# Operands ordered by first use, a residual load moved in the queue, and a ring of four weight slots, in a two-layer decoder trunk

## The chip, the cores and the metric

The kernel runs on one core of a Trainium2 chip. The metric is the device time of one execution in microseconds (us). The core has five engines that run their own instruction streams and wait for each other by semaphores: TensorE (PE, matmuls and transposes, into PSUM), VectorE (DVE), ScalarE (ACT), GpSimd (POOL), and SyncE (SP), which here only issues DMAs, in the order of its program.

## What is computed

Two layers, on 1024 prompt positions and 8 x 8 sample positions (1088 rows of 1024 features), all in fp32:

```python
for l in range(2):
    h = x @ w_in                                   # 1024 -> 1792
    A = gelu(h_u) * (tril(W_s) @ LN(gelu(h_v)) + b)  # gMLP gating in chunks of 128, 8 heads
    B = sliding-window attention, 8 query heads / 2 kv heads, rotary, sinks
    x = LayerNorm(alpha * x + concat(A, B) @ w_out)
    up = x @ w_up                                  # 1024 -> 2 * 2816
    g, u = causal depthwise conv, width 3 (up)
    x = LayerNorm(alpha * x + (gelu(g) * u) @ w_down)   # 2816 -> 1024
```

Outputs are x and the updated key, value, conv and gMLP rows.

## The kernel before

fp32 products are made of three passes with rounded operands: each operand is split into a high half (ACT copies it to fp32r) and a low half (DVE or POOL subtracts the high half from the original), and PE does high x high, high x low and low x high. So each weight tile passes through DMA, ACT, DVE or POOL, and PE. The order of every engine is written out by hand; an instruction behind a wait waits too.

A layer has these stages.

- Input projection, w_in. SP loads pairs of weight tiles (`pair_in`, 1 MB), ACT makes the high half (`hi_in`, L770), POOL the low one (`lo_in`, L682). The first two tiles are multiplied in `two_chunks` (L1702) for each third of the columns. The columns come from row tiles that PE turns (`turn_x`, L1660) into the banks that `x_bank` names (L336), and ACT and DVE evict from there as high and low half (`x_hi` L794, `x_lo` L1153). In layer 0 the odd tiles have banks of their own; in layer 1 all use banks 6 and 7, so each waits for the eviction of the one before. `hi_in` of layer 1 stands at the end of ACT's loop over the down-projection (L1143), behind the square roots of the last norms (`deviation`).
- Gating and attention, which the change doesn't touch.
- Output projection, w_out. Row tiles in three groups, `C3 = [(0,1,2), (3,4,8), (5,6,7)]`. For each of 8 weight rows kk, PE multiplies the three tiles of the group with the high half (two passes) and then the low half. The last two weight rows of a group (kk = 6, 7) are handled tile by tile, so that the three tiles are done one after the other (L1942 to L1953); before the first of them PE waits for both high and both low halves, and in group 0 does the sample values (`samp_values`). DVE adds the residual (`summed`, L1165), which SP brings with `x_rows` (L456); the one of the third tile is issued between weight rows (L626). Then the norm: `deviation` (ACT), `scaled` (DVE), `normal` (ACT), PE turns the tile (`turn_z`), ACT and DVE evict it with gain and bias (`turned`).
- Up-projection, w_up, in 22 slices. Each is seven products of 4 k-tiles by 544 columns (a Strassen-like scheme: 7 products for 8), in the order B_11, B_12, B_S2, B_S1, B_S3, B_22, B_S4. Their right operands are `ba` and `bt`: the x tiles and four sums t1 to t4 of tile halves, each as high and low. For a tile of 4 to 7 they are made in three parts: part 0 is t1 and t2 (used by S2 and S1), part 1 is t3 and t4 (S3 and 22), part 2 the tile itself (S4). ACT's `operand_hi` (L836) does the three parts of a tile together, DVE's `operands` (L1255) turns a tile, makes its sums and its three low parts, and goes to the next tile. The weight blocks go through `block_hi` (ACT), `lo_up` and `sum_up` (POOL; from slice 1 on some through `block_lo`, DVE). After B_11, ACT copies the product out of PSUM (`snap`, L882); for slice 0 this waits for the last low part, because the place it is written to still holds the x tiles. DVE joins the products (`joined`, L1274).
- Down-projection, w_down: three groups of three row tiles in order, each of 22 units (k-tiles), so 66 units d. `down_hi`/`down_lo` split the weight row into slot `dn_slot(d)` (L141), `act_hi`/`act_lo` split the activations, which come back from HBM (`araw<-a_scr`). The last two units of a group are handled tile by tile. Slots 0 and 1 are also the places of the w_in tiles of the next layer and, like slot 3, of blocks of the up-projection. ACT's `down_hi` waits for the unit that used the slot before:

```python
def dn_slot(d):
    return d % 4 if d < DNU - 2 else d - (DNU - 4)      # DNU = 66: units 64, 65 in slots 2, 3
...
name, count = used_d(l, d - (4 if d < DNU - 2 else 2))
```

SP's queue begins with the four constants, x tiles 0 to 2, the first w_in pair and the other x tiles (L393, L516 to L522).

Of the kernel before, what the change touches and what calls it, by code (L numbers as in the profile page):

```python
# [10 lines left out]
ALU = mybir.AluOpType  # L11
# [113 lines left out]
def xo_n(l, t, part):  # L125

    n = sum(parts(u) for u in CORD[:CORD.index(t)])
    return l * sum(parts(u) for u in CORD) + n + part + 1


def ts_n(l, t, i):

    n = sum(0 if u < HK else 4 if u < NB else 8 for u in CORD[:CORD.index(t)])
    return l * 4 * (HK + 2) + n + i + 1
# [6 lines left out]
def dn_slot(d):  # L141

    return d % 4 if d < DNU - 2 else d - (DNU - 4)
# [10 lines left out]
def trunk(nc, x_prompt, x_sample, cache_k, cache_v, cache_conv, w_in, gmlp_g, gmlp_b, w_spatial,  # L154
# [4 lines left out]
    with ctx:  # L159
# [53 lines left out]
        bh_off = [hi_off[i // 2] + 2048 * (i % 2) for i in range(4)] + [e_off + 2048 * i for i in range(3)]  # L213
        bl_off = [lo_off[i // 2] + 2048 * (i % 2) for i in range(4)] + [e_off + 6144 + 2048 * i for i in range(3)]
# [60 lines left out]
        gu = [at(f"gu{i}", [P, 2, UWX], u_off + 9152 * i) for i in range(2)]  # L275
        hg = [at(f"hg{i}", [P, CV], u_off + 18304 + 4416 * i) for i in range(2)]
# [18 lines left out]
        for n in ("const_landed x_landed0 x_landed1 x_landed2 x_landed3 x_tr x_hi x_lo par_landed cs_landed bd_landed bd_zero par_tr "  # L295
# [63 lines left out]
        def half(f, which, h):  # L359

            return gu[f % 2][:, which, HW_ * h:HW_ * h + HW_].rearrange("p (b n) -> p b n", b=2)

# [29 lines left out]
        def _(sp):  # L392
            for dst, src in ((ident[:], c_ident), (mask[:], c_mask), (smask[:], c_smask), (selS[0:HEADS, :], c_sel)):  # L393
                sp.dma_start(dst, src).then_inc(S["const_landed"], 16)
# [121 lines left out]
            for b in range(NB + 1):  # L516
# [3 lines left out]
                if b == 3:  # L520
                    pair_in(0, 0)
                sp.dma_start(xin[b % XS][0:tokens(b), :], src).then_inc(S[f"x_landed{b % XS}"], 16)  # L522

            def body(l):
# [3 lines left out]
                else:  # L528
                    sp.wait_ge(S["z_tr"], l * NTOK)
                    sp.wait_ge(S["z_out2"], 48 * l)  # L530
                    for dst, src in ((mask[:], c_mask), (smask[:], c_smask), (selS[0:HEADS, :], c_sel)):
                        sp.dma_start(dst, src).then_inc(S["const_landed"], 16)
# [82 lines left out]
                for cache, o in ((cache_k, o_ks), (cache_v, o_vs)):  # L615
                    sp.dma_start(o[l, :, 0:WINDOW - DS].rearrange("b s k d -> b s (k d)"),
                                 cache[l, :, DS:WINDOW].rearrange("b s k d -> b s (k d)")).then_inc(S["c_out"], 16)
                for g in range(3):
                    for kk in range(KD):
# [6 lines left out]
                        if g == 0 and kk == 5:  # L626
# [1477 lines left out]
```

## Time and profile before

| | |
|---|---|
| median of 3 runs | 2487.73 us (2486.95 to 2490.62) |
| profiled execution | 2495.53 us, span 2493.8 us |
| PE busy | 2291.3 us, 92% |
| DVE / ACT / POOL busy | 68% / 39% / 29% |
| mean granted PE clock | 0.964 |

The busy share of PE in 40 equal slices, with its granted clock (tenths of full speed; slices of 62 us) and the DMA engines' share:

```profile
PE   6999888699999999999979998886999999999997
...
PEclk9999989799999999999989999898999999999998
DMA  5311135122222225665442212451222222255762
```

Busy counts a matmul that runs at half clock as fully busy. The slices in which PE is below 9 are the start, the attention and output projection of each layer, the turn between the layers (slice 21) and the end. The up-projection of a layer takes about 450 us, its down-projection about 290.

### The profile page before, as it was taken

The numbers are of one execution on the slowest core, as the hardware profiler recorded it, in microseconds if no ns is written. First come the engines' busy times: TensorE is split into PE (matmuls) and PEld (weight loads), VectorE is DVE, ScalarE is ACT, GpSimd is POOL, SyncE is SP. The second block draws the span as 40 slices with busy tenths as digits, with TensorE's granted clock in tenths as the row PEclk, the third lists the DMA queues.
The fourth block names the chain that finished last, engine by engine and source line by source line (L and its number), as shares of the span: only waits on it lengthen the run. The fifth ranks groups of instructions, "written<-read, shape, count | busy, mean of one in ns | idle before, by whom it ended". The sixth has DMA issues, their size and how long they took to land.

```text
span 2493.8 us, 36152 instructions
## 1 busy us (share of the span) xinstructions
PE 2291.3 (92%) x14396; PEld 2038.8 (82%) x14396; DVE 1683.4 (68%) x2092; ACT 983.0 (39%) x1773; POOL 716.6 (29%) x396
## 2 busy tenths in 40 slices
PE   6999888699999999999979998886999999999997
PEld 6997566699999998787779976666999999977875
DVE  1469736677777776776535797376777777757665
ACT  2226625434343344333222266344433444433331
POOL 1110134344444440220211112344444444302211
PEclk9999989799999999999989999898999999999998
DMA  5311135122222225665442212451222222255762
GB/s 143 88 53 38 60 118 170 59 68 65 80 79 80 79 63 179 233 213 194 131 108 62 49 39 85 123 152 43 80 80 79 63 71 79 96 204 197 238 201 80
DMA packets 207975, 269.52 MB, mean 108 GB/s; under 512 B 31952, under 2 KB 166584, under 8 KB 207736
## 3 DMA queue, kind: packets, MB, share of 16 engines
q1 hardware_dynamic: 207808, 267.21, 35.0%
q8 instruction: 115, 1.88, 0.3%
q14 instruction: 52, 0.43, 0.1%
HBM read 217.39 MB, written 46.13 MB: 106 GB/s over the span
## 4 chain that ended last, share of the span: by engine, by line
PE 57%; DVE 19%; ACT 6%; issue 5%; DMA 5%; POOL 5%; SPq 2%; DVEq 0%; ACTq 0%; POOLq 0%
PE ps L1970 21%; PE ps L1690 15%; PE ps L1656 8%; PE ps L1912 6%; DMA wblk<-in_w_up 3%; DVE rl L1340 2%; POOL bl L697 2%; SPq L510 2%; PE ps L1715 1%; DMA wrow<-in_w_down 1%; POOL wblk L705 1%; DVE bl L1272 1%; ACT bh L880 1%; DVE al L1347 1%; DVE Sb L1486 1%
## 5 line engine op out<-in xcount | busy, mean ns | idle before, releaser
L1970 PE MATMUL ps<-bt,bh 128*128 128x272 f32 x3520 | 595.1, 291 | 32.0 <-issue 23.8
L1970 PEld LDWEIGHTS ps<-bt,bh 128*128 128x128 f32 x3520 | 500.4, 190 | 39.6 <-issue 25.4
L880 ACT ACTIVATE bh<-wblk 128x512 fp32r<-128x512 f32 x308 | 183.5, 624 | 547.2 <-POOL wblk L709 234.0
L1970 PE MATMUL ps<-bt,bl 128*128 128x272 f32 x1760 | 365.6, 289 | 0.0
L1272 DVE TENSOR_TENSOR bl<-wblk,bh 128x512 fp32r<-128x512 f32 x210 | 165.4, 804 | 192.2 <-ACT bh L880 192.2
L1970 PEld LDWEIGHTS ps<-bt,bl 128*128 128x128 f32 x1760 | 276.9, 190 | 0.0
L1690 PE MATMUL ps<-rh,ah 128*128 128x512 f32 (+1 forms) x792 | 249.5, 396 | 22.1 <-DVE rzd L1175 6.8
L697 POOL TENSOR_TENSOR bl<-wblk,bh 128x512 fp32r<-128x512 f32 x98 | 166.8, 1707 | 321.4 <-ACT bh L880 321.4
L1690 PE MATMUL ps<-rh,al 128*128 128x512 f32 (+1 forms) x792 | 246.6, 393 | 0.0
L1690 PE MATMUL ps<-rl,ah 128*128 128x512 f32 (+1 forms) x792 | 246.0, 392 | 0.0
L1970 PE MATMUL ps<-ba,bh 128*128 128x272 f32 x1408 | 237.5, 291 | 6.7 <-POOL bl L697 1.7
L1340 DVE TENSOR_TENSOR rl<-wrow,rh 128x1024 fp32r<-128x1024 f32 x132 | 189.4, 1435 | 68.8 <-ACT rh L938 68.8
L1970 PEld LDWEIGHTS ps<-ba,bh 128*128 128x128 f32 x1408 | 198.4, 188 | 15.5 <-DVE gu L1295 13.0
L693 POOL TENSOR_TENSOR rl<-wrow,rh 128x1024 fp32r<-128x1024 f32 x48 | 116.9, 2438 | 307.6 <-ACT rh L792 191.5
L1690 PEld LDWEIGHTS ps<-rh,ah 128*128 128x128 f32 (+1 forms) x792 | 143.1, 184 | 64.6 <-issue 12.5
L1656 PE MATMUL ps<-xh,wh 128*128 128x384 f32 (+1 forms) x576 | 193.9, 337 | 0.9 <-POOL wl L685 0.9
L1656 PE MATMUL ps<-xh,wl 128*128 128x384 f32 (+1 forms) x576 | 190.0, 330 | 0.0
L1656 PE MATMUL ps<-xl,wh 128*128 128x384 f32 (+1 forms) x576 | 189.8, 330 | 0.0
L1912 PE MATMUL ps<-rh,mrow 128*128 128x512 f32 (+1 forms) x576 | 155.7, 413 | 34.2 <-DVE rzc L1175 22.5
L722 POOL TENSOR_TENSOR rzd<-rzd,gain 128x1024 f32<-128x1024 f32 (+1 forms) x18 | 50.6, 2809 | 438.3 <-DMA rzd<-z_scr 438.3
L1690 PEld LDWEIGHTS ps<-rl,ah 128*128 128x128 f32 (+1 forms) x792 | 145.4, 184 | 37.0
L1690 PEld LDWEIGHTS ps<-rh,al 128*128 128x128 f32 (+1 forms) x792 | 145.2, 183 | 36.4
(220 smaller groups left out, 4077.5 us busy)
## 6 DMA issues: line engine op xcount, KB each, us to landing
wrow<-in_w_down SPq DMA_DIRECT2D x132, 512.0 KB, 4.4
wblk<-in_w_up SPq DMA_DIRECT2D x88, 512.0 KB, 5.3
a_scr<-hg SPq DMA_DIRECT2D x44, 552.0 KB, 3.5
araw<-a_scr SPq DMA_DIRECT2D x88, 192.0 KB, 3.6
wrow<-in_w_out SPq DMA_DIRECT2D x48, 256.0 KB, 4.9
wrow<-in_w_out SPq DMA_DIRECT2D x24, 512.0 KB, 3.4
wraw<-in_w_in SPq DMA_DIRECT2D x10, 1024.0 KB, 6.1
z_scr<-rzc SPq DMA_DIRECT2D x16, 512.0 KB, 3.8
```

The source lines that it names most:

```text
L510: sp.dma_start(o_cs[l, :, r, c0:c0 + 256], src[10 + r:90:10]).then_inc(S["rows_out"], 16)
L693: pool.tensor_tensor(rl[c % 2][:], wrow[(c + 2) % 4][:], rh[c % 2][:].bitcast(F32), ALU.subtract).then_inc(S["w_lo"], 1)
L697: pool.tensor_tensor(bl[b][:], block_of(f, b), bh[b][:].bitcast(F32), ALU.subtract).then_inc(S["u_lop"], 1)
L705: pool.tensor_tensor(a21, a21, a22, ALU.add).then_inc(S["u_sum"], 1)
L722: pool.tensor_tensor(rz, rz, gain[0][0:tokens(t), :], ALU.mult).then_inc(S["xp1"], 1)
L880: act.activation(bh[b][:], block_of(f, b), ACT.Copy).then_inc(S["u_hi"], 1)
L1272: dve.tensor_tensor(bl[b][:], block_of(f, b), bh[b][:].bitcast(F32), ALU.subtract).then_inc(S["u_lov"], 1)
L1340: dve.tensor_tensor(rl[s][:], wrow[(d + 2) % 4][:], rh[s][:].bitcast(F32), ALU.subtract).then_inc(S["d_lo"], 1)
L1656: e = nc.tensor.matmul(out, lhs, rhs, start=(m == 0), stop=(m == n - 1))
L1690: e = nc.tensor.matmul(ps[0:q, 2 * i + half, :], lhs, rhs[:, 512 * half:512 * half + 512], start=(first and m == 0), stop=(final and m == 2))
L1912: e = nc.tensor.matmul(ps[0:tokens(t), 2 * i + n, :], m_tile(t, KORD[kk], low), right[:, 512 * n:512 * n + 512], start=start, stop=stop)
L1970: e = nc.tensor.matmul(out[:, n, :], lhs, rhs[:, HW_ // 2 * n:HW_ // 2 * n + HW_ // 2], start=(k == 0 and m == 0), stop=(k == HK - 1 and m ...
```

## The change

- `dn_slot` becomes a ring: unit d has slot (d + 2) % 4, and every `down_hi` from unit 4 on waits for unit d - 4. Units 0 and 1 get slots 2 and 3, so they wait for other blocks of the last slice, and ACT and DVE split them later in their programs. The places of three weight blocks (`bh`, `bl` 4 to 6) are interleaved for this.
- ACT's two `hi_in` of the next layer stand before the last unit's square roots and wait for units 62 and 63.
- The last three tiles' operands (5, 6, 7): ACT and DVE do part 0 of each tile as it comes, and parts 1 and 2 of all three after the last; DVE makes t3 there too (`sum_third`). The copy of slice 0's first product goes to a place of its own (`s1t`) and doesn't wait for them; the block S4, whose place overlaps it, waits for the joint that reads it last.
- `x_rows` of the third tile is issued before the output projection's weight rows 8 and on.
- The tail of a group in the output projection: for each tile first both high halves, then the two low halves; each is waited for where it is used. The sample values come after the first tile.
- At the start: only the identity is loaded ahead of x0; the first w_in pair is issued behind x0; the other constants after the x tiles. ACT converts weights between x tiles. In both layers tile 7 is turned into banks 2 and 5.

```diff
 def dn_slot(d):
-    return d % 4 if d < DNU - 2 else d - (DNU - 4)
+    return (d + 2) % 4
...
+        s1t = at("s1t", [P, HW_], e_off + 9600)
...
         def x_bank(l, t):
+            if t == 7:
+                return ps[:, 2:6:3, :]
             if l == 0 and t % 2:
-                return ps[:, 4:6, :] if t < 6 else ps[:, 2:6:3, :]
+                return ps[:, 4:6, :]
             return ps[:, 6:8, :]
...
         def _(sp):
-            for dst, src in ((ident[:], c_ident), (mask[:], c_mask), (smask[:], c_smask), (selS[0:HEADS, :], c_sel)):
-                sp.dma_start(dst, src).then_inc(S["const_landed"], 16)
+            sp.dma_start(ident[:], c_ident).then_inc(S["id_landed"], 16)
...
-                if b == 3:
+                if b == 1:
                     pair_in(0, 0)
...
+                x_rows(l, C3[0][2])
                 for g in range(3):
                     for kk in range(KD):
...
-                        if g == 0 and kk == 5:
-                            x_rows(l, C3[0][2])
...
                 elif l:
-                    act.wait_ge(S["d_used"], used_d(l - 1, DNU - 6 + j)[1])
+                    act.wait_ge(S["d_used"], used_d(l - 1, DNU - 4 + j)[1])
...
-                    name, count = "u_p", 7 * (l * FT + FT - 1) + (2, 4, 6, 7)[d]
-                else:
-                    name, count = used_d(l, d - (4 if d < DNU - 2 else 2))
+                    name, count = "u_p", 7 * (l * FT + FT - 1) + (6, 6, 2, 4)[d]
+                else:
+                    name, count = used_d(l, d - 4)
...
                 if l == 0:
-                    for t in range(3):
-                        x_hi(0, t)
+                    x_hi(0, 0)
                     hi_in(0, 0)
+                    x_hi(0, 1)
                     hi_in(0, 1)
-                    for t in range(3, NTOK):
+                    for t in range(2, NTOK):
                         x_hi(0, t)
...
                 turned(l, t0)
+                operand_hi(l, t0, 0)
                 block_hi(l, 0, B_S2)
-                operand_hi(l, t0)
                 turned(l, t1)
+                operand_hi(l, t1, 0)
                 block_hi(l, 0, B_S1)
-                operand_hi(l, t1)
                 turned(l, t2)
-                operand_hi(l, t2)
-                snap(l, 0)
-                for b in (B_22, B_S3, B_S4):
-                    block_hi(l, 0, b)
+                operand_hi(l, t2, 0)
+                for part in (1, 2):
+                    for t in C3[2]:
+                        operand_hi(l, t, part)
+                    if part == 1:
+                        snap(l, 0)
+                        block_hi(l, 0, B_22)
+                block_hi(l, 0, B_S3)
...
                     if f:
                         snap(l, f)
+                    else:
+                        block_hi(l, 0, B_S4)
...
-                        down_hi(l, 0)
                         act_hi(l, 0)
-                        down_hi(l, 1)
                         act_hi(l, 1)
-                        down_hi(l, 2)
+                        for d in range(3):
+                            down_hi(l, d)
...
                 for d in range(DNU):
                     g, k = divmod(d, FT)
+                    if d == DNU - 1 and l < DEPTH - 1:
+                        hi_in(l + 1, 0)
+                        hi_in(l + 1, 1)
...
+                for t in C3[2]:
+                    sum_third(l, t)
+                for part in (1, 2):
+                    for t in C3[2]:
+                        operand_lo(l, t, part)
...
-                    high = [out_hi(KD * g + kk) for kk in (KD - 2, KD - 1)]
-                    low = [out_lo(KD * g + kk) for kk in (KD - 2, KD - 1)]
-                    if g == 0:
-                        samp_values()
                     for i in range(3):
-                        for m, kk in enumerate((KD - 2, KD - 1)):
-                            out_part(g, i, kk, 0, high[m])
-                            out_part(g, i, kk, 1, high[m])
-                            e = out_part(g, i, kk, 0, low[m], stop=(m == 1))
-                            if m == 0 and i == 2:
-                                e.then_inc(S["c_used"], 1)
-                        e.then_inc(S["c_done"], 1)
+                        for kk in (KD - 2, KD - 1):
+                            high = out_hi(KD * g + kk)
+                            out_part(g, i, kk, 0, high)
+                            out_part(g, i, kk, 1, high)
+                        e = out_part(g, i, KD - 2, 0, out_lo(KD * g + KD - 2))
+                        if i == 2:
+                            e.then_inc(S["c_used"], 1)
+                        out_part(g, i, KD - 1, 0, out_lo(KD * g + KD - 1), stop=True).then_inc(S["c_done"], 1)
+                        if g == 0 and i == 0:
+                            samp_values()
```

## Rows read from the trace of the kernel before

**Rows 1.** Waits of PE over the whole run: total us, times, longest.

```profile
PE ps L1970 <- issue: 23.8, 4, 9.5
...
PE ps L1912 <- DVE rzc L1175: 22.5, 4, 9.9
```

**Rows 2.** Busy by window: PE, PEld, DVE, ACT, POOL, then PEclk, DMA, GB/s.

```profile
8.00:10.00 2.00, 2.00 (x11) 2.00 (x11) 0.00 (x0) 0.22 (x1) 0.00 (x0) 1.00 1.04 386
1241.00:1243.00 2.00, 2.00 (x6) 1.52 (x6) 0.00 (x0) 0.00 (x0) 0.00 (x0) 0.50 0.00 0
```

**Rows 3.** PE timeline, turn of the layers: start, us, what, [idle before <- releaser].

```profile
1235.27 0.63 PE L1690 MATMUL ps<-rh,al 128*64 128x512 f32 x2
1238.93 1.19 PE L1690 MATMUL ps<-rh,ah 128*128 128x512 f32 x2 [3.03 <-DVE al L1350]
...
1256.95 0.66 PE L1715 MATMUL ps<-xh,wh 128*128 128x384 f32 x1 [6.71 <-POOL wl L685]
...
1276.05 1.03 PE L1673 MATMUL ps<-ident,rzd 128*128 128x128 f32 x8
...
1285.73 0.64 PE L1715 MATMUL ps<-xh,wh 128*128 128x320 f32 x1 [0.69 <-ACT xh L797]
```

**Rows 4.** Timelines of ACT, POOL, DVE and SP at the same turn.

```profile
1253.35 1.99 ACT L781 ACTIVATE wh<-wraw 128x1024 fp32r<-128x1024 f32 x2
...
1254.47 5.66 POOL L685 TENSOR_TENSOR wl<-wraw,wh 128x1024 fp32r<-128x1024 f32 x2 [41.28 <-ACT wh L781]
...
1254.44 3.45 DVE L1200 SCALAR_TENSOR_TENSOR rzd<-rzd,rst,gain 128x1024 f32<-128x1024 f32 x1
...
1222.39 0.38 SPq L404 DMA_DIRECT2D wraw<-in_w_in  x1
```

**Rows 5.** Timeline near the end of layer 1, PE and DVE.

```profile
2469.37 0.69 PE L1690 MATMUL ps<-rh,ah 128*128 128x512 f32 x2 [3.03 <-DVE al L1350]
...
2474.06 1.22 DVE L1175 SCALAR_TENSOR_TENSOR rzd<-rzd,ps 128x1024 f32<-128x1024 f32 x1 [4.84 <-PE ps L1690]
```

**Rows 6.** Timeline of the start of layer 0, PE and ACT.

```profile
7.75 3.65 PE L1673 MATMUL ps<-ident,xin 128*128 128x128 f32 x16 [7.75 <-DMA xin<-in_x_prompt]
...
20.02 0.66 PE L1715 MATMUL ps<-xh,wh 128*128 128x384 f32 x1 [4.57 <-POOL wl L685]
...
43.95 1.91 PE L1673 MATMUL ps<-ident,xin 128*128 128x128 f32 x16
...
48.82 0.42 PE L1715 MATMUL ps<-xh,wh 128*128 128x320 f32 x1 [0.69 <-ACT xh L797]
...
16.40 1.99 ACT L781 ACTIVATE wh<-wraw 128x1024 fp32r<-128x1024 f32 x2
```

**Rows 7.** Timelines of PE, DVE and ACT in layer 0's output projection.

```profile
330.55 0.27 PE L1893 MATMUL ps<-pTs,vc 128*64 128x32 f32 x2 [1.90 <-POOL rl L693]
362.17 1.97 PE L1912 MATMUL ps<-rh,mrow 128*64 128x512 f32 x4 [9.88 <-DVE rzc L1175]
393.39 1.16 PE L1912 MATMUL ps<-rh,mrow 128*128 128x512 f32 x4 [2.64 <-POOL rl L693]
...
360.89 1.22 DVE L1175 SCALAR_TENSOR_TENSOR rzc<-rzc,ps 128x1024 f32<-128x1024 f32 x1 [5.36 <-DMA rzc<-in_x_prompt]
...
352.50 1.28 ACT L820 ACT_TABLE_LOAD   x1
```

**Rows 8.** Timelines of PE and DVE, first slice of layer 0's up-projection.

```profile
474.01 1.24 PE L1970 MATMUL ps<-bt,bh 128*128 128x272 f32 x4 [9.50 <-issue]
...
490.80 1.25 PE L1970 MATMUL ps<-bt,bh 128*128 128x272 f32 x4 [2.69 <-issue]
...
465.61 2.40 DVE L1253 TENSOR_TENSOR bt<-btf,bt 128x1024 fp32r<-128x1024 f32 x2
```

**Rows 9.** Timelines of PE and ACT where layer 0's down-projection begins.

```profile
957.40 0.70 PE L1690 MATMUL ps<-rh,ah 128*128 128x512 f32 x2 [1.28 <-DVE gu L1295]
...
954.55 0.52 ACT L948 ACTIVATE ah<-araw 128x384 fp32r<-128x384 f32 x1 [9.32 <-DMA araw<-a_scr]
```

More of the change, by code:

```diff
@@ L125, in xo_n @@
 def xo_n(l, t, part):
-    n = sum(parts(u) for u in CORD[:CORD.index(t)])
-    return l * sum(parts(u) for u in CORD) + n + part + 1
-def ts_n(l, t, i):
-    n = sum(0 if u < HK else 4 if u < NB else 8 for u in CORD[:CORD.index(t)])
-    return l * 4 * (HK + 2) + n + i + 1
+    last = C3[2]
+    n = sum(parts(u) for u in CORD[:6])
+    if t in last:
+        n += 3 * part + last.index(t)
+    else:
+        n = sum(parts(u) for u in CORD[:CORD.index(t)]) + part
+    return l * sum(parts(u) for u in CORD) + n + 1
+def ts_n(l, t, i):
+    last = C3[2]
+    n = sum(0 if u < HK else 4 if u < NB else 8 for u in CORD[:CORD.index(t)]) + i
+    if t in last:
+        n = 12 + (9 + last.index(t) if i == 3 else 3 * last.index(t) + i)
+    return l * 4 * (HK + 2) + n + 1
 def up_bank(f, product):
@@ L361, in half, with first @@
             return gu[f % 2][:, which, HW_ * h:HW_ * h + HW_].rearrange("p (b n) -> p b n", b=2)
+        def first(f):
+            return s1t[:].rearrange("p (b n) -> p b n", b=2) if f == 0 else half(f, 1, 1)
         def up_ps(f, product):
@@ L843, in operand_hi @@
                     act.wait_ge(S["kv_out"], 32 * (l + 1))
-                elif t == HK:
+                elif t == HK and part == 0:
                     act.wait_ge(S["c_done"], l * NTOK + 6)
@@ L860, in operand_hi, with operands_hi @@
                     e.then_inc(S["xo_hi"], 1)
+                else:
                     act.activation(bt[:, 0:4, HT:HW_], mix[:, HK:KD, SEQ + HS:T], ACT.Copy).then_inc(S["xo_hi"], 1)
+            def operands_hi(l, t):
+                for part in range(parts(t)):
+                    operand_hi(l, t, part)
             def block_hi(l, f, b):
@@ L888, in snap @@
                     act.wait_ge(S["rows_pe"], n - 1)
-                elif f == 0:
-                    act.wait_ge(S["xo_lo"], xo_n(l, CORD[-1], 2))
-                act.activation(half(f, 1, 1), up_ps(f, B_11), ACT.Copy).then_inc(S["snap_g"], 1)
+                act.activation(first(f), up_ps(f, B_11), ACT.Copy).then_inc(S["snap_g"], 1)
             def moves(l, f):
@@ L1209, in turned, with sum_third @@
                 e.then_inc(S["xf_dv"], 1)
+            def sum_third(l, t):
+                cols = first_cols(t)
+                right = slice(HT + cols.start, HT + cols.stop)
+                dve.tensor_tensor(btf[:, 32:36, cols], mix[:, HK:KD, right], mix[:, 0:HK, right], ALU.subtract).then_inc(S["t_sum"], 1)
             def operand_sums(l, t):
@@ L1262, in operands @@
                     operand_lo(l, t, 0)
-                    operand_lo(l, t, 1)
-                    operand_lo(l, t, 2)
+                    if t not in C3[2]:
+                        operand_lo(l, t, 1)
+                        operand_lo(l, t, 2)
                 else:
@@ L1283, in joined @@
                     dve.wait_ge(S["snap_g"], n + 1)
-                    dve.tensor_tensor(g1, u2, done(B_12), ALU.add).then_inc(S["u_c11"], 1)
+                    dve.tensor_tensor(g1, first(f), done(B_12), ALU.add).then_inc(S["u_c11"], 1)
                 elif out == "u2":
-                    dve.tensor_tensor(u1, u2, done(B_S2), ALU.add).then_inc(S["u_u2"], 1)
+                    dve.tensor_tensor(u1, first(f), done(B_S2), ALU.add).then_inc(S["u_u2"], 1)
                 elif out == "v":
```

68 lines of the change are left out of this document (37 added, 31 removed).

## The prediction

> **What bounds the kernel now.** I read the waits of the matrix engine (PE) first, then its timeline at each seam between two stages, then the timelines of ScalarE (ACT), VectorE (DVE) and GpSimd (POOL) at the same seams. Inside a stage PE has almost no gap; its idle time stands at the seams. The two largest kinds that the change touches [rows 1]: 23.8 us before L1970 for the operands of the up-projection and 22.5 before L1912 for the layer norm of a residual tile; the others come below, at their place. A gap costs twice: behind one of about 3 us the granted clock is 0.50, that is 1.2 GHz instead of 2.4 [rows 2], until PE has worked some microseconds. A 512-column matmul then goes from about 0.23 to 0.43 us. All sums below are against the profiled execution (2495.53 us, span 2493.8); it lies 7.8 us above the median of the runs, 2487.73. What the sum removes I take off the median.
>
> **1. The turn from layer 0 to layer 1: -20 us.** The last two weight slots of the down-projection were reused after two units instead of four, so the conversion of unit 64 waits for unit 62 and PE stands for 3.03 us, from 1235.9 to 1238.93, and then runs at half clock [rows 2, 3]. In the ring of four both are converted before the tail. The tail is 36 matmuls of 0.227 us (three row tiles, two units, six each): 8.2 us, so it ends at 1244.1. The first two weight tiles of w_in then have to be there. Before, ACT converts them at 1253.35, behind the last square roots, and POOL splits the first by 1256.8, when PE starts [rows 3, 4]. Their slots are freed by units 62 and 63, at 1231.8 and 1235.9 (a unit is 18 matmuls, 4.1 us); the change puts the two conversions before the square roots. With ACT's 1.0 and POOL's 2.4 us the second low half is ready at 1239.5, before 1244.1: PE goes on without a gap, 12.85 us earlier than 1256.95. The two products that follow took 19.1 us (1256.95 to 1276.05 [rows 3]), a part of it at half clock; at full clock 96 matmuls of 0.174 are 16.7: 2.4 less. The three transposes and evictions after them took 9.68 us (1276.05 to 1285.73 [rows 3]) and took 4.87 in layer 0, where tile 7 already has its own banks (43.95 to 48.82 [rows 6]): 4.8 less. Together 12.85 + 2.4 + 4.8 = 20. The rest of the chain keeps up: DVE's last norms move with the tail, by about 6, and lose the stretched steps below, and are needed only at 1261. Bounds: -22, and -14 if the square roots and y rows that the queues carry hold the second weight pair.
>
> DVE's step at 1254.44 took 3.45 us where its like took 1.3, beside POOL's split of these weights [rows 4]; the change moves that split beside DVE's preparation of the last units. The Trainium skill, "SBUF — State Buffer", on the shared port pair, says that a VectorE instruction with two SBUF inputs and a GpSimd instruction that reads SBUF exclude each other for a whole instruction. The stretched row agrees with it. It is the third rival below.
>
> **2. The end: -4.9 us.** The same ring removes the 3.03 us in layer 1. There DVE's chain of norms sets the end. It began at 2474.06, when PE, held to 2469.37, had done the first tile [rows 5]. Without the gap PE is at this tile at 2466.34, and has it 12 matmuls later, at 2469.1. The rest of the chain is as long as before. Bounds -4 and -6.
>
> **3. The start: -6 us.** PE gets x0 at 7.75 and the first weights at 20.02; ACT converts the weights only after three x tiles, at 16.40 [rows 6]. Three constants (0.46 MB, three issues) leave the front of the queue, and the 1 MB of weights goes ahead of x1 and x2. At 386 GB/s [rows 2], with x0 about 4 us after an issue at 1.3: x0 at about 5.3, weights 8.1, x1 9.4, x2 10.8. ACT: x0 done 9.4 (the table load, 1.3, is still there), weights 10.4; POOL 12.8; x1 12.3; second weights 13.2; PE's third transposes 11.3 to 13.2, x2 converted at 14.3. That is when PE can start: 5.7 us earlier, and part of the half clock goes. The moved constants add 1.3 us of issues in the queue before the parameters, which PE wants some 10 us later. Bounds -3 (x1 and x2 land late behind the weights) and -7.5.
>
> **4. Output projection, first seam: -6.7 us in each layer.** The residual rows of the third tile were issued behind six weight rows; DVE waits 5.36 us for their landing and PE 9.88 [rows 7]. Moved ahead, they are held by one wait, for the sample softmax's mask (done at 320), with eight weight DMAs queued behind; those then go 2.5 us later, for weights wanted at 349. No one waits for that. What ends last next is ACT: two weight conversions, an eviction, a split, the table load at 352.50 [rows 7], the root, then DVE: scale, split, sum, ready at 7.1 us after the end of the group. It is now 12.0 after it (350.2 to 362.17). So 4.9 is gained and 4.4 of gap stays. The tail of the group before it no longer waits for both low halves: the 1.90 before the sample values [rows 7] goes, as 8 matmuls on the high halves (1.8 us) come first. 4.9 + 1.8 = 6.7. Bounds -5 and -8.
>
> **5. Its other seams: -2.1 us in each layer.** The same reordering takes 2.64 to 0.3 [rows 7] and some half clock, 2.9 in all. But the low half of the last but one weight is now read at the very end of each tile; its slot comes free one matmul pair before the group's end instead of three, so ACT's next conversions, and the roots behind them, are 0.5 to 0.9 later. The layer norm of the third tile is there what PE waits for. Net -2.1, bounds -1 and -3.5. At the third tail DVE's operand chain is what is late, so of 3 us only 1.4 in layer 0 and nothing in layer 1 counts (in part 6).
>
> **6. First slice of the up-projection: -8.2 us in both.** PE waits 9.50 before the third product and 2.69 before the last [rows 8]. The DVE work does not shrink: per tile two low parts of 2.40 together and one of 0.7 [rows 8], and the sum of 0.7; the change only puts those that the third product doesn't need behind the last transposes. Walking the three engines from the first eviction with these durations, the third product can start after 17.0 us instead of 22.3. Then another chain ends last: ACT's conversion of block 22, POOL's low half, POOL's sum, ACT, POOL, 5.5 us to the fifth product; it starts 3.5 earlier, since its first step stands behind part 1 and not behind all parts. The last product follows 9 us later, with a gap of 2.9. So 3.4 in each layer, plus 1.4 in layer 0. Bounds: 0 (the chain of POOL keeps its place) and -11.
>
> **7. Up to down-projection: +4 us.** The new ring gives unit 0 slot 2, and ACT converts it after both activations, the first of which comes by DMA at 954.55 [rows 9]. DVE then does its low half at 958.2, after the third joint, and PE starts at 959.5 instead of 957.40. The gap, 1.28 before [rows 9], becomes 3.4 in layer 0 and 2.7 in layer 1, with half clock behind it. The first unit ends 0.8 later, plus 1.2 for the clock: +2 in each, since the two later starts inside the unit, for the joints, don't wait any more. Bounds +1 and +7.
>
> **Sum.** -20 - 4.9 - 6 - 13.4 - 4.2 - 8.2 + 4 = -52.7. On the median: 2435.0. The bounds all on one side would give -26 and -69; independent of each other, as their causes are, they give about -43 to -62, so 2426 to 2445.
>
> **Rivals.** (a) The turn gives its tail but not its start: the weights for layer 1 are held, by their landing or by ACT's order, and PE still waits. For it: the pair is issued only at the end of the down-projection; against it: it is issued at 1222.39 [rows 4], 9 us before its use, and 1 MB at 386 GB/s is 2.7 us, with some 4 more from issue to landing. Then 12.85 - 6.1 + 2.4 = 9 are missing, and other seams fall short by as much again: 2453. Chance 0.11. (b) Slower: the ring. If in the moved slots each of the 132 down units had to wait for a slot, 0.40 us a unit eats all 52.7, and beyond that the kernel is slower; at 0.5 us it takes 2501. Against it: 64 of 66 units already reuse their slot after four, and only the number of the slot changes. 0.02. (c) The shared port: POOL's two splits (2.4 us each) catch the low halves of unit 65, which the tail needs; up to 2.4 us of gap and 2.7 of half clock return: 2440. 0.10, and inside the range. (d) The reordered operands bring nothing, since the work is the same and only POOL's chain counts: 2443. 0.10, inside the range too. (e) More than forecast, since less half clock follows each smaller gap: under 2424. 0.05.
>
> **How the numbers follow.** The forecast with its own bounds has 0.62, (a) 0.11, (b) 0.02, (c) and (d) 0.10 each, (e) 0.05. The range is stretched past 2426 to 2445 for sizes misjudged at six seams: 2424 to 2452. A measurement of this kernel tells about 0.2% (5 us) from no change. Faster by more 0.96, within it 0.02, slower by more 0.02.
>
> **What would show it.** In the new profile: no wait before L1690 in the tails, no wait before the first L1715 of layer 1; first products at about 14.3; the gap at the residual of the third tile 4 to 5 us, not 10; third product of slice 0 earlier by 5, last by 3.4; a gap of about 3 us before the first down unit. I am wrong if PE still waits at the turn, if x1 and x2 land after 12 us, or if a stage without an edit gets longer.

## The result and the profile after

The changed kernel takes 2433.82 us (median of 4 runs, 2430.51 to 2435.85), the kernel before 2488.61 beside it (4 runs, 2486.95 to 2490.62): ratio 0.9776, 95% interval 0.9763 to 0.9788, or 54.8 us less. Forecast were 2435.0 and 52.7 less. The profiled execution took 2430.51, span 2428.8, at a mean granted clock of 0.972. It lies 65.0 below the profiled one of before, whose own time was above its median; the difference is taken stage by stage below.

Engine totals and the granted clock on the page of the changed kernel:

```profile
PE 2279.8 (94%) x14396; PEld 2034.1 (84%) x14396; DVE 1681.7 (69%) x2092; ACT 983.6 (40%) x1773; POOL 719.1 (30%) x396
...
PEclk9999889899999999999999998898999999999999
```

Waits of PE in the changed kernel (total us, times, longest):

```profile
PE ps L2014 <- issue: 19.5, 4, 7.6
PE ps L1956 <- DVE rzc L1206: 11.8, 4, 4.4
...
PE ps L2014 <- POOL bl L716: 8.3, 4, 2.2
...
PE ps L1734 <- DVE rl L1378: 5.4, 2, 3.6
```

The wait for the residual tile has halved (22.5 in [rows 1]). That for the operands of the up-projection has only gone from 23.8 to 19.5, and one of 8.3 for POOL's low halves stands beside it (1.9 in the kernel before). The 5.4 is new: it is the wait before unit 0, which is part 7 of the prediction.

The turn of the layers in the changed kernel, timelines of PE, POOL and DVE:

```profile
1221.67 0.33 PE L1759 MATMUL ps<-xh,wh 128*128 128x384 f32 x1
...
1238.34 1.91 PE L1717 MATMUL ps<-ident,rzd 128*128 128x128 f32 x16
...
1243.20 0.41 PE L1759 MATMUL ps<-xh,wh 128*128 128x320 f32 x1 [0.69 <-ACT xh L816]
...
1211.22 2.40 POOL L704 TENSOR_TENSOR wl<-wraw,wh 128x1024 fp32r<-128x1024 f32 x1 [21.13 <-ACT wh L800]
1214.87 2.40 POOL L704 TENSOR_TENSOR wl<-wraw,wh 128x1024 fp32r<-128x1024 f32 x1 [1.25 <-ACT wh L800]
...
1226.03 1.28 DVE L1231 SCALAR_TENSOR_TENSOR rzd<-rzd,rst,gain 128x1024 f32<-128x1024 f32 x1
```

There is no wait in the tail and none before the first product (3.03 and 6.71 in [rows 3]). The two products take 16.67 (19.1 before), turn and eviction 4.86 (9.68). DVE's steps keep their 1.3 where one was stretched to 3.45 [rows 4].

First group of the output projection, and the seam behind the second, in layer 0 of the changed kernel (PE timeline):

```profile
320.92 2.11 PE L1956 MATMUL ps<-rh,mrow 128*128 128x512 f32 x8
...
348.31 1.97 PE L1956 MATMUL ps<-rh,mrow 128*64 128x512 f32 x4 [4.41 <-DVE rzc L1206]
379.74 0.73 PE L1956 MATMUL ps<-rl,mrow 128*128 128x512 f32 x2 [0.29 <-POOL rl L712]
```

The eight matmuls on high halves at 320.92 run where PE waited 1.90 before. 9.88 became 4.41, 2.64 became 0.29 [rows 7].

Slice 0 of the up-projection in layer 0, changed kernel, PE and DVE. The first row is the first product, the next three are the third, fifth and last. The DVE rows are the low half of the next slice's block S2 and the joint v behind it:

```profile
428.47 0.73 PE L2014 MATMUL ps<-ba,bh 128*128 128x272 f32 x4 [2.05 <-POOL bl L716]
...
452.15 1.25 PE L2014 MATMUL ps<-bt,bh 128*128 128x272 f32 x4 [7.57 <-issue]
462.54 0.73 PE L2014 MATMUL ps<-bt,bh 128*128 128x272 f32 x4 [2.06 <-POOL bl L716]
472.49 0.74 PE L2014 MATMUL ps<-bt,bh 128*128 128x272 f32 x4 [2.18 <-issue]
...
470.49 1.27 DVE L1310 TENSOR_TENSOR bl<-wblk,bh 128x512 fp32r<-128x512 f32 x1 [7.96 <-ACT bh L908]
471.68 0.71 DVE L1327 TENSOR_TENSOR gu<-gu,ps 128x544 f32<-128x544 f32 x1
```

In the kernel before, the first and the fifth product:

```profile
446.08 0.74 PE L1970 MATMUL ps<-ba,bh 128*128 128x272 f32 x4 [0.83 <-POOL bl L697]
...
481.85 0.74 PE L1970 MATMUL ps<-bt,bh 128*128 128x272 f32 x4 [0.23 <-POOL bl L697]
```

The last product starts 44.0 us after the first. Before, 446.08 to 490.80 [rows 8], it was 44.7. The third has come 4.2 nearer, the fifth 1.7, the last only 0.7.

The first unit of the down-projection and the start of its second group, PE, changed kernel:

```profile
940.54 0.73 PE L1734 MATMUL ps<-rh,ah 128*128 128x512 f32 x2 [3.64 <-DVE rl L1378]
1037.08 0.73 PE L1734 MATMUL ps<-rh,ah 128*128 128x512 f32 x2 [1.90 <-DVE rzd L1206]
```

With the same cuts in both traces (first product of w_in, of w_out, of w_up, of w_down, in each layer; then PE's last matmul) the 65.0 us of the two profiled executions divide as follows:

| stage | layer 0 | layer 1 |
|---|---|---|
| before the first product of w_in | -5.5 | (in the turn) |
| w_in, gating, attention | -2.8 | -10.8 |
| output projection | -9.3 | -10.0 |
| up-projection | +0.8 | -0.3 |
| down-projection (layer 0: to the next layer's first product) | -18.4 | -8.7 |

Of the 18.4, the tail and the turn have 13.0, the first group 3.0 and the second 2.4. Of the 10.8, the two products and the turned tile have 7.2 (16.67 for 19.1, 4.86 for 9.68); the other 3.6 fall in code that nobody touched.

### The profile page after: what moved, and what is told of

Read it like the earlier page. It is cut to its first block, busy times and chain, and to the rows that moved or that the text cites. A ratio compares the mean times of both kernels' runs of the same rounds, so it can differ in the third digit from the quotient of the medians.

```text
span 2428.8 us, 36140 instructions
## 1 busy us (share of the span) xinstructions
PE 2279.8 (94%) x14396; PEld 2034.1 (84%) x14396; DVE 1681.7 (69%) x2092; ACT 983.6 (40%) x1773; POOL 719.1 (30%) x396
## 4 chain that ended last, share of the span: by engine, by line
PE 62%; DVE 17%; ACT 6%; issue 5%; POOL 4%; DMA 3%; SPq 2%; DVEq 0%; ACTq 0%; POOLq 0%
PE ps L2014 23%; PE ps L1734 18%; PE ps L1698 8%; PE ps L1956 6%; DMA wblk<-in_w_up 2%; POOL bl L716 2%; POOL wblk L724 1%; ACT bh L908 1%; SPq L529 1%; PE ps L1759 1%; DVE bl L1310 1%; DVE Sb L1524 1%; DVE bnst L1210 1%; DVE rl L1378 1%; PE ps L1853 1%
## 5 line engine op out<-in xcount | busy, mean ns | idle before, releaser
L2014 PE MATMUL ps<-bt,bh 128*128 128x272 f32 x3520 | 598.3, 293 | 29.3 <-issue 19.5
L1734 PE MATMUL ps<-rh,ah 128*128 128x512 f32 (+1 forms) x792 | 246.3, 392 | 13.7 <-DVE rzd L1206 6.8
```

The costliest lines, as they stand in the source:

```text
L1734: e = nc.tensor.matmul(ps[0:q, 2 * i + half, :], lhs, rhs[:, 512 * half:512 * half + 512], start=(first and m == 0), stop=(final and m == 2))
L2014: e = nc.tensor.matmul(out[:, n, :], lhs, rhs[:, HW_ // 2 * n:HW_ // 2 * n + HW_ // 2], start=(k == 0 and m == 0), stop=(k == HK - 1 and m ...
```

## The experiments

Each undoes one part of the changed kernel, or goes a step further. Times are medians of 4 runs (5 for the last). The kernel before ran beside them on each chip, at 2488.63, 2489.84, 2491.93 and 2491.43 us; the ratios to it are compared where the chips differ. By the intervals a difference of less than about 4 us between two of these kernels isn't clear.

**The changed kernel again.**

> The changed kernel once more, unedited, as the mark for the three beside it. The two profiled executions so far lie 65 us apart and the medians 54.8. Theory: about 10 us of a single execution is where the half-clock stretches in the untouched attention fall, so this profile may lie anywhere from 2430 to 2440 and the median at 2432 to 2436. Rival: the larger distance is the change's own, because a shift in time carries over to later stages; then the profile lies within 1 us of 2430.5 again, with the same waits.

Measured: 2433.01 (2430.03 to 2435.72), ratio 0.9779 (0.9762 to 0.9795). Its profiled execution took 2430.03, span 2428.3, and the stretch with gating and attention is as long as in the first in both layers, to 0.03 us. So the rival is nearer: the two profiled executions agree, in the span to 0.5 us. But each is the fastest of its four. The other six take 2432.79 to 2435.85, at granted clocks of 0.969 to 0.971 against 0.972, so its time is not the same in every execution. This comes back in the section on the hardware.

**The ring, undone at its end.**

```python
def dn_slot(d): return d % 4 if d < DNU - 2 else d - (DNU - 4)
...
name, count = "u_p", 7 * (l * FT + FT - 1) + (2, 4, 6, 6)[d]
...
name, count = used_d(l, d - (4 if d < DNU - 2 else 2))
```

ACT's two `hi_in` of the next layer wait for the last units of slots 0 and 1 under these numbers, 60 and 61.

> The last two units of the down-projection reuse their slots after two units again; the slots' numbers go back with them; the place of the two w_in conversions stays. Theory (parts 1 and 2): one wait of about 3.0 us before unit 64 in each layer, and 1.2 to 1.9 of half clock behind it: +8.5 to +10 on the median, about 2443. Rival: the tail's gain was the smaller part and the norms hide it, +3 to +5. A rival on the ring's price: the moved slot numbers cost something in every unit, then this kernel would come out faster than the changed one.

Measured: 2444.18 (2442.11 to 2447.12), +11.2. The two tails in its profile: DVE's row of the low half and POOL's beside it in layer 0, and PE's row in each layer:

```profile
1213.24 2.39 DVE L1388 TENSOR_TENSOR al<-araw,ah 128x64 fp32r<-128x64 f32 x1
...
1213.20 4.67 POOL L704 TENSOR_TENSOR wl<-wraw,wh 128x1024 fp32r<-128x1024 f32 x2 [26.17 <-ACT wh L800]
...
1215.77 1.19 PE L1734 MATMUL ps<-rh,ah 128*128 128x512 f32 x2 [5.20 <-DVE al L1388]
...
2418.85 1.19 PE L1734 MATMUL ps<-rh,ah 128*128 128x512 f32 x2 [3.03 <-DVE al L1388]
```

The wait of 3.03 returns in layer 1 alone. In layer 0 it is 5.20, since DVE's step there takes 2.39 and not its usual 0.22. POOL's split of the next layer's weights begins at 1213.20 beside it. That is the collision of rival (c), and its price, 2.2 us of wait. The 11.2 lie above the expected 8.5 to 10, which had no collision in them. In the changed kernel unit 65's last low half is done at 1210.79, before the split at 1211.22, and the collision doesn't happen. The Trainium skill, "SBUF — State Buffer", on the shared port pair, says that such a pair of instructions takes turns as a whole; the two rows agree, 2.39 being the length of one split (2.40).

**The weights of the next layer, late again.**

```python
# behind the last root again, not at d == DNU - 1
hi_in(l + 1, 0); hi_in(l + 1, 1)
```

> The two conversions of layer 1's first w_in tiles go back behind the last square roots; the ring stays. Theory (part 1): the last root waits for the last norm at about 1224.7, ACT and POOL then take 1.0 and 2.4, so PE starts layer 1 at about 1228.4 instead of 1221.5, with half clock in its first two products: +9, from 6.9 and 2.4; about 2443. Rival: another chain is late at that place anyhow (the norms' transposes), +3 or less.

Measured: 2440.82 (2440.16 to 2441.79), +7.8. The first product of layer 1 in its profile:

```profile
1228.07 0.66 PE L1759 MATMUL ps<-xh,wh 128*128 128x384 f32 x1 [6.71 <-POOL wl L704]
```

It is the wait of before [rows 3], to the last digit, and in the profile the way from the first product of w_down to this one is 9.0 us longer than in the changed kernel, the 9 expected. The median shows 7.8 of it.

**The residual rows, late again.**

```python
if g == 0 and kk == 5: x_rows(l, C3[0][2])
```

> The residual rows of the third tile are issued behind six weight rows again; everything else stays. Theory (part 4): the gap before the third tile at the first seam is 9.3 to 9.9 us instead of 4.4, in both layers: +5 to +5.5 each, 2444. Rival: with the tail's new order the landing is partly hidden behind the sample values and only half of it comes back: +5, 2439.

Measured: 2445.27 (2442.17 to 2448.48), +12.3. The wait at the first seam is 9.62 in layer 0 and 9.52 in layer 1:

```profile
353.42 1.97 PE L1957 MATMUL ps<-rh,mrow 128*64 128x512 f32 x4 [9.62 <-DVE rzc L1207]
```

So 5.2 and 5.1 of wait come back. The output projections themselves are only 2.2 and 4.0 longer, since PE spends less time at half clock behind the other waits: it is busy for 123.4 us in layer 0, where the changed kernel has 126.4 for as many matmuls. The rest of the 14.4 between the two profiled executions lies mostly in the untouched stages from w_in to attention (2.1 and 2.6) and in the first down-projection (2.8). The median's 12.3 is therefore no price of the rows alone.

**The order of the last two weights, undone.**

```python
high = [out_hi(KD * g + kk) for kk in (6, 7)]; low = [out_lo(KD * g + kk) for kk in (6, 7)]
if g == 0: samp_values()
```

> Only the order of the two last weights in each tail of the output projection is put back (both high and both low halves waited for before the first tile, sample values ahead of it). Theory (parts 4 and 5): 1.9 at the first seam and 2.1 at each of the other two returns where it is not hidden: +3 to +7 for both layers, about 2439. Rival: the gain there is given back because the slot comes free later (ACT and the roots 0.5 to 0.9 later): within 2 of the changed kernel.

Measured: 2443.47 (2442.37 to 2445.62), ratio 0.9814: 0.0035 above the changed kernel, 8.7 us. The tail of the third group and the first product behind it, layer 0:

```profile
425.44 1.17 PE L1956 MATMUL ps<-rh,mrow 128*128 128x512 f32 x4 [2.71 <-POOL rl L712]
434.85 0.74 PE L2015 MATMUL ps<-ba,bh 128*128 128x272 f32 x4 [0.83 <-POOL bl L716]
```

Four waits of 2.6 to 2.7 and two of 1.87 are back. At the third seam a part was indeed given back in the changed kernel: its first product waits 2.05, and 0.83 here. The 8.7 lie above the expected 3 to 7. In the profile the two output projections are 2.8 and 3.6 longer, within it; another 3.7 and 2.8 fall in the untouched stages ahead of them.

**The start, undone.**

```python
if b == 3: pair_in(0, 0)            # and the three constants ahead of x0
x_hi(0, 0); x_hi(0, 1); x_hi(0, 2); hi_in(0, 0); hi_in(0, 1)
```

> Only the start is put back: three constants ahead of the x tiles, the first pair of weights behind x2, ACT converting it behind three x tiles. Theory (part 3): first product at 20.0 instead of 14.55, and a part of the half clock: +5.5 to +7, 2440. Rival: the later wait for x1 and the work behind it take the gain back: +3 or less.

Measured: 2442.07 (2440.55 to 2445.76), ratio 0.9810, 7.7 us more. Its first product is at 18.41, where the changed kernel has 14.55. That is not the 20.02 of before: x0 landed at 7.02 and not at 7.75, and the third tile's transposes took 1.07 and not 1.94. The stage behind it is 4.7 us longer: its first matmuls follow each other every 0.32 us, at half clock, where the changed kernel has 0.17.

**The operands' order, undone.**

```python
for t in C3[2]: turned(l, t); operands_hi(l, t)       # all three parts of a tile before the next
snap(l, 0); block_hi(l, 0, B_22)
```

> Only the order of the operands of the last three token tiles is put back (all parts of a tile before the next, snapshot and block 22 behind all); the snapshot's own buffer stays. Theory (part 6): third product of slice 0 later by 5.3, last by 3 to 4 in each layer: +6 to +8, 2441. Rival (d): GpSimd's chain of sums sets the end of the slice and nothing changes: within 2.

Measured: 2436.25 (2433.11 to 2439.11), ratio 0.9784 (0.9769 to 0.9799) against 0.9779 (0.9762 to 0.9795): 1.2 us, less than the intervals. Its rows for slice 0 in layer 0 (first, third and last product, and DVE's low half of the next slice's block S2):

```profile
427.07 0.73 PE L1993 MATMUL ps<-ba,bh 128*128 128x272 f32 x4 [2.05 <-POOL bl L706]
...
455.66 1.24 PE L1993 MATMUL ps<-bt,bh 128*128 128x272 f32 x4 [9.50 <-issue]
470.98 0.73 PE L1993 MATMUL ps<-bt,bh 128*128 128x272 f32 x4 [1.76 <-issue]
...
468.97 1.28 DVE L1294 TENSOR_TENSOR bl<-wblk,bh 128x512 fp32r<-128x512 f32 x1 [8.01 <-ACT bh L898]
```

The third product starts 4.9 later than in the changed kernel, counted from the first, and the last one no later at all: 43.9 against 44.0. The last product needs the joint v. In DVE's queue v stands behind the low half of the next slice's block S2, which begins 41.9 us after the first product here and 42.0 in the changed kernel. It hangs on a chain that the new order didn't shorten: the joint u2, ACT's block S4, POOL's low halves and sums. The new order puts u2 behind all the low halves (461.82 in the changed kernel, 460.24 here, 33.4 and 33.2 after the first product).

Less idle time is no gain here either. Over the whole up-projection, changed kernel and this one (PE, PEld, DVE, ACT, POOL busy, clock, DMA, GB/s):

```profile
428.47:940.54 512.07, 487.02 (x3763) 479.16 (x3763) 380.20 (x433) 209.65 (x354) 212.66 (x136) 0.98 0.25 75
```

```profile
427.07:939.20 512.13, 484.05 (x3762) 475.56 (x3762) 378.79 (x433) 209.56 (x354) 210.84 (x136) 0.98 0.25 75
```

With the new order PE is idle 3.0 us less (25.05 for 28.08) and busy 3.0 us more for the same matmuls, because it waits three times in slice 0 (7.57, 2.06, 2.18) instead of twice (9.50, 1.76) and runs at half clock behind each of the three, but not behind the 1.76.

**Slice 0, a step further.**

```python
block_hi(l, 0, B_22)                       # ACT, ahead of parts 1 and 2
joined(l, 0, "c11"); joined(l, 0, "u2")    # DVE, behind part 1
joined(l, 0, "v")                          # DVE, ahead of block_lo(l, 1, B_S2)
```

> A step further in slice 0, from the profile of the changed kernel: ACT converts block 22 ahead of the third operands, DVE makes c11 and u2 ahead of the last low halves and v ahead of the next slice's block. Theory: the waits of 2.06 before the fifth product and of 2.18 before the last go, with 1.3 and 2 of half clock: -4 to -7.5 in each layer, 2419 to 2426. Rival: block 22's low half on GpSimd slows DVE's low halves beside it and the third product comes later by 1 to 2: no gain.

Measured: 2432.53 (2427.74 to 2433.91), ratio 0.9766, 3.2 us less by the ratio, which is inside the intervals. Both waits went but for 0.3 us, and another came one product later: slice 1 now waits 2.27 for the joint c22, which stands behind the same low half. Slice 1 still begins 3.8 us nearer to the first product (44.7 against 48.5). In the following slices PE waits for v 17 times, 7.5 us in all (12 times and 5.0 in the changed kernel). The whole up-projection is only 1.1 and 1.2 us shorter. So most of what is won in slice 0 is given back in the slices behind it.

**DVE's queue in every slice.**

```python
joined(l, f, "v"); product(l, f - 1); joined(l, f, "u3"); joined(l, f, "c22")
block_lo(l, f + 1, B_S2); block_lo(l, f + 1, B_S1); rows_evac(l, f - 1)
joined(l, f, "c21"); block_lo(l, f + 1, B_22)
```

> The changed kernel with another order in VectorE's queue in every slice of the up-projection: the joints v, u3 and c22 ahead of the low halves of the next slice's blocks S2 and S1, which wait for GpSimd's sums. Nothing else moves. Theory: the operand order brought nothing because this queue sets the pace, in slice 0 and behind it: a slice takes 22.0 us on average where PE alone needs 21.3. Then 21 slices lose about 0.6 each in both layers, 25, and slice 0 loses its wait of 2.18 with the half clock behind it, 3 in each: 2400 to 2408. Rival: the loop over ACT, GpSimd's sums and the low half of block 22 sets the pace; then the 22.0 stay, and only slice 0's part comes, 2428 or more.

Measured: 2396.56 (2396.55 to 2397.55), ratio 0.9624 (0.9608 to 0.9640), 3.4 us below the expected 2400 to 2408. Windows of 100 us in the up-projection (PE, PEld, DVE, ACT, POOL busy, clock, DMA), first the changed kernel, then this one:

```profile
600.00:700.00 100.00, 99.00 (x775) 97.04 (x774) 74.69 (x84) 39.73 (x70) 41.32 (x27) 1.00 0.26 77
```

```profile
600.00:700.00 100.00, 100.00 (x802) 100.00 (x801) 77.23 (x83) 42.79 (x74) 49.30 (x29) 1.00 0.26 77
```

PE's busy share of 99% had looked like a bound. It isn't: the number of matmuls in the same 100 us goes from 775 to 802. The busy share hides this because the record of a matmul is longer than its turn: 0.29 us on average, while without waits the next one starts after 0.125 (100 us over 802). So the record covers the first part of each short wait. A slice takes 21.27 us where it took 21.92 (transposes of one slice to those of the next, over 19 slices; 21.97 in the kernel before). That is 13.7 in each layer over 21 slices; the wait before the last product of slice 0 goes too, with its half clock.

**The same, with the operands' old order.**

> The run beside it (label loop) with the operands of the last three tiles in the old order again. Theory: with VectorE's queue no longer the bound, the order of the operands counts, and undoing it costs about what part 6 gave it, 3.4 in each layer: 5 to 8 above its neighbour, where it was 2 to 3 in the changed kernel. Rival: the end of slice 0 hangs on GpSimd's chain of low halves and sums all the same, then the two are within 2 of each other.

Measured: 2397.75 (2397.05 to 2399.37), ratio 0.9628 (0.9614 to 0.9643), 1.2 above its neighbour. The rival's number holds. In layer 0, slice 1 (its transposes) is reached 50.8 us after the first product with the new order and 52.2 with the old: the order of the operands is worth about 1.4 in a layer in the profile, not 3.4, even where DVE's queue is in nobody's way. What is left then with the new order is the wait for POOL's low half of block S3, 2.16. PE is idle 2.8 us less than with the old order, and half of that is lost again at half clock.

**Two seams.**

```python
m_hi(l, 5); hi_out(l, 9)                                     # ACT, sample outputs ahead of weight 9
summed(l, 0, t2); m_lo(l, 5); scaled(l, 0, t0)               # DVE, third tile first
act_cols(l, d)                                               # SP, ahead of the last product's rows
name, count = "u_p", 7 * (l * FT + FT - 1) + (5, 6, 2, 4)[d] # ACT, unit 0 after S3
```

> Two seams of the changed kernel a step further. First seam of the output projection: the sample outputs and their high half ahead of weight 9 on ACT, VectorE sums the third tile ahead of the scale of the first; gap of 4.41 becomes about 0.6: -4 to -5.5 in each layer. Up to down-projection: the activations' loads go ahead of the last product's rows, unit 0's weights wait for the product S3 alone, its low half goes ahead of the last joints; the gaps of 3.64 and 1.72 go, with the half clock: -3 to -5 in layer 0, -2 to -3 in layer 1. Together 2417 to 2422. Rival to the second: the first unit then waits for the joints and half of it stays, 2424.

Measured: 2425.03 (2424.57 to 2425.31), ratio 0.9737, against 0.9779: 10.5 less, and short of what was expected. PE's first seam in layer 0 and a unit of the first down-projection group:

```profile
344.20 1.11 PE L1957 MATMUL ps<-rh,mrow 128*64 128x512 f32 x4 [1.01 <-DVE mrow L1193]
...
993.59 0.70 PE L1735 MATMUL ps<-rh,ah 128*128 128x512 f32 x2 [1.15 <-DVE al L1385]
```

The output projection became 5.5 and 5.0 shorter. At the down-projection the gap went in both layers, but in layer 0 waits of 0.22 and 1.15 for DVE came back inside the group. The larger one comes from POOL. DVE's row in front of it, and POOL's beside it:

```profile
990.71 2.73 DVE L1385 TENSOR_TENSOR al<-araw,ah 128x384 fp32r<-128x384 f32 x1
...
989.66 3.37 POOL L741 TENSOR_TENSOR rzd<-rzd,gain 128x1024 f32<-128x1024 f32 x1
```

Six DVE steps in a row, 0.55 and 1.2 us elsewhere, take 2.7 and 3.4 here, as long as POOL prepares the residual of three tiles. The changed kernel has the same six stretched steps, but its PE comes later and doesn't wait for them in layer 0. From the last product of slice 21 to the second group, 3.3 us were gained in layer 0 and 1.6 in layer 1. The span of the profiled execution is only 5.4 shorter, for the untouched stages from w_in to attention are 1.1 and 4.5 longer than in the changed kernel.

**All of it together.**

> The changed kernel with the queue order of label loop, the two seams of label edges, and slice 0 as in label imp_slice0 (block 22 converted ahead of the third operands, c11 and u2 ahead of the last low halves). Theory: the parts add up, since with a slice at 21.27 us nothing behind a seam takes its gain back: 2396.6 for the loop, minus 8.8 to 10 for the seams, minus 2.2 and about 1.3 of half clock in each layer's slice 0 for the wait before the fifth product: 2378 to 2383. Rival: the seams' gains and slice 0's fall into the same waits, 2386 or more.

Measured: 2380.00 (2378.35 to 2386.93), ratio 0.9554 (0.9541 to 0.9567): by the ratios 2.3% below the changed kernel and 4.5% below the kernel before. The parts add up, once the slice has no wait left: it takes 21.27 here too.

## Why the prediction came out right, point by point

| part | forecast | measured | by |
|---|---|---|---|
| 1, 2: the tails | -6.1 -4.9 | -11.2 | ring undone |
| 1: next layer's weights | -9.1 | -7.8 | weights late |
| 1: tile 7's banks | -4.8 | -4.8 | profile, turn to product |
| 3: start | -6 | -7.7 | start undone |
| 4: residual rows | -9.8 | -12.3 | rows late |
| 4, 5, 6: order of the last weights | -9.2 | -8.7 | order undone |
| 6: operands' order | -6.8 | -1.2 | order undone, twice |
| 7: up to down | +4 | -3.2 | profile |
| sum | -52.7 | -56.9 | (result: -54.8) |

(The forecast's 9.2 are 1.8 and 2.1 in each layer and the 1.4 of layer 0; the 9.1 are 12.85 + 2.4 less the 6.1 that rival (a) keeps. By the intervals, each undone part is uncertain by about 4 us; the tails' 11.2 hold the 2.2 of the collision.)

The total is right to 1.2 us, but two of its terms are wrong by 5.6 and 7.2, in opposite directions. That they cancel is luck; with either alone the total would have been 6 or 7 us off, still inside the range. The times of the single parts also carry several us of half clock in stages without an edit, so a term of the table is not surer than that. The banks of tile 7 and part 7 were not undone by themselves and rest on the profile.

**Part 1, the turn**: right in its mechanism and size. First product 1221.67; from the third group's start to it 90.22 us against 103.21, 12.99 less where the text had 12.85. Rival (a) did not come: no wait is left. Rival (c) did not come either, though the run with the ring undone showed that it was real.

**Part 2, the end**: the wait before the last tile is gone. From the second group to PE's last matmul it is 4.9 less, as forecast; the other 3.7 of the stage's -8.7 lie in its first group (part 7).

**Part 3, the start**: x0 at 5.45 (5.3 forecast), x1 at 9.61 (9.4), first product at 14.55 (14.3). By the undone start it was worth 7.7, a little over its bound of 7.5.

**Part 4**: the gap that stays was forecast as 4.4 and is 4.41. The experiment gives the rows more than the 9.8 forecast, though the wait itself grew by just 5.2 and 5.1 and the two stages by 2.2 and 4.0; the rest fell in other stages.

**Part 5**: 2.64 to 0.3 forecast, 0.29 measured. Waits of 0.76 for ACT's next conversion are new; they come from the slot that is free later, as the text had it.

**Part 6, the step that failed**: the walk to the third product was right. It starts 17.4 us after the first eviction (17.0 forecast, 22.3 before). Two steps behind it failed, in layer 0:

- The fifth product came 1.7 nearer to the first and not 3.5. POOL's low half of block 22 begins 2.7 earlier (28.3 us after the first product for 30.9), and POOL's three steps from there take 5.65 us instead of 4.66, since they now run beside DVE's low halves (1.69, 1.62 and 1.53 for 1.28, 1.30 and 1.30).
- From the fifth to the last product the text took 9 us, "with a gap of 2.9"; it is 9.95. It stopped its walk at PE's products and left out DVE's queue behind them. The last product waits for v; v stands behind an instruction for the next slice; and that one waits for ACT and POOL.

The text also counted no half clock behind the waits that stay, though there are now three of them. Rival (d) named the outcome, nothing gained, and POOL's chain, which is a part of the reason; at a chance of 0.10 it was given too little, and its 2443 was missed only because of part 7.

**Part 7, mis-sized with the wrong sign**: the gap came out as forecast in layer 0 (3.64 for 3.4; 1.72 for 2.7 in layer 1). But from the last product of slice 21 to the second group, layer 0 got 0.6 shorter and layer 1 2.6 shorter. The kernel before had four more waits inside that group (0.53, 0.90, 0.44 and 1.05 in layer 0) for a joint of DVE and its low halves; the changed kernel has none of them in layer 0, and one of 1.57 in layer 1. The text counted only the joints among those that the later start hides. DVE has a fixed piece of work there, and PE's idle time lies in front of it or inside it. The wait of 1.05 is the one beside POOL's residual steps that came back in the run with two seams.

**The rivals on the other side**: (b), the ring slower in each unit, is out. The run with the slots' old numbers was slower, not faster.

## What to carry to other kernels

A walk along the chain of one stage must end at the next stage's first instruction and follow the queues of all engines, not only PE's products: an instruction that waits for the next iteration's data holds everything behind it in its queue. Where every iteration of a loop has a short wait of this kind, gains ahead of the loop are given back inside it, and putting the joints ahead of the next iteration's preparation is worth more (about 38 us here) than the new order at the seam in front (1.2). One long wait cut into several short ones gains less than the idle time shows, when each of them is followed by half clock: 3.0 us less idle and 3.0 us more busy in the same up-projection. A busy share of 99% doesn't show that an engine is the bound; count its instructions in equal windows.

## What the runs showed of the hardware

How long PE stays at half clock differs between kernels in code that nobody touched. From the first product of w_in to that of w_out in layer 0, the kernels of this study, but for the two with the old start, have the same instructions in the same order. The changed kernel takes 276.47 and, run again, 276.50; with the tail order undone it is 280.15, with the weights late 277.81. In layer 1 the changed kernel has 268.17 and 268.16, and the others with the same code there 269.7 to 272.8. The waits differ by at most 1.6 us in these stages, and not in step with the times. What differs is the mean granted clock: 0.97 over the 268.2 us, and 0.94 over the 272.8 of the kernel with the old operands' order. The output projection does it too. In layer 0 it takes 134.05 with the ring undone and 134.04 with the weights late, at a mean clock of 0.96, and 137.46 in the changed kernel at 0.93, with 11.0 us of waits in each.

So edits elsewhere go with shifts of up to 4.6 us in a stage, as large as most terms of the sum, and they explain a part of what the undone parts show over their waits. The one kernel that was profiled twice repeated its values, but its other executions differ among themselves by 3 us. Whether such a shift belongs to the edit in every execution isn't shown, and what decides how long the clock stays at 0.50 I did not settle.

A DVE step of 0.22 us was held for 2.39, the length of one POOL instruction beside it. In the down-projection DVE's steps of 0.55 us take 2.7 in a row beside POOL's residual steps. And POOL is held too: its low half of 128x512 took 1.37 us in the kernel with the old operands' order and 1.69 in the changed one, where it begins beside DVE's low halves.
